# Folding the tokens of a real input twice before its Fourier transform, and writing the outputs in pairs k and N-k

## The reference, cut to what matters

```python
def fourier_mix(u):
    b, n, _ = u.shape
    u32 = u.reshape(b, n, F_GROUPS, F_CH).astype(jnp.float32)
    f = jnp.fft.fftn(u32, axes=(1, 3), norm="ortho").real
    return f.reshape(b, n, F_WIDTH).astype(u.dtype)
```

## Time and profile before

| | |
|---|---|
| median of three runs | 2781.35 us |
| the profiled execution | 2780.91 us |
| its span, first to last instruction | 2779.1 us |
| busy TensorE (matmul) | 2700.9 us, 97% |
| busy VectorE, ScalarE, GpSimd | 1643.2, 1018.4, 968.4 us |
| mean granted TensorE clock | 0.994 |

### The profile page before, as it was taken

How to read it: one execution, slowest core, us unless ns; L and a number is a source line. 1 busy time by engine, 2 the same in 40 slices (tenths; PEclk the granted TensorE clock), 3 DMA queues, 4 the chain that set the end, 5 groups by cost and what they waited for, 6 DMA issues and landing times.

```text
span 2779.1 us, 39815 instructions
## 1 busy us (share of the span) xinstructions
PE 2700.9 (97%) x16386; PEld 2214.9 (80%) x16386; DVE 1643.2 (59%) x1803; ACT 1018.4 (37%) x1377; POOL 968.4 (35%) x596
## 2 busy tenths in 40 slices
PE   7999999999999999999999999999899999999997
PEld 4878877888788888788888888888777888888885
DVE  6479118986963455755436666666869443444436
ACT  4332216773533343445453222222334222222223
POOL 0111115203397873222222111111134744455552
PEclk9999999999999999999999999999999999999998
DMA  7211450012412124111121111111122111111112
GB/s 234 76 31 39 126 185 1 1 65 73 137 46 61 46 61 134 54 48 46 53 57 39 39 39 39 39 39 39 32 77 73 48 46 46 61 61 54 51 31 101
DMA packets 260432, 175.71 MB, mean 63 GB/s; under 512 B 5792, under 2 KB 252960, under 8 KB 259104
## 3 DMA queue, kind: packets, MB, share of 16 engines
q1 hardware_dynamic: 258816, 169.69, 20.3%
q10 hardware_dynamic: 1440, 3.51, 0.3%
HBM read 164.79 MB, written 8.39 MB: 62 GB/s over the span
## 4 chain that ended last, share of the span: by engine, by line
PE 72%; issue 13%; DVE 6%; POOL 4%; ACT 3%; DVEq 1%; DMA 0%; POOLq 0%; SPq 0%; ACTq 0%
PE PS L2134 11%; PE PS L2136 10%; PE PS L2135 10%; PE PS L2537 10%; PE PS L2538 10%; PE PS L2539 10%; POOL Wlo L601 3%; ACT exp L1006 1%; DVE acol L1677 1%; PE PS L2311 1%; PE PS L2641 1%; PE PS L2648 1%; PE PS L2232 1%; PE PS L2448 1%; PE PS L2677 1%
## 5 line engine op out<-in xcount | busy, mean ns | idle before, releaser
L601 POOL TENSOR_TENSOR Wlo<-Wraw,Whi 128x1024 fp32r<-128x1024 f32 (+1 forms) x140 | 337.1, 2408 | 1150.5 <-ACT Whi L795 1150.5
L2134 PE MATMUL PS<-Bh,Whi 128*128 128x512 f32 x1216 | 486.4, 400 | 6.9 <-DVE Bl L1438 2.5
L2136 PE MATMUL PS<-Bh,Wlo 128*128 128x512 f32 x1216 | 475.1, 391 | 0.0
L2135 PE MATMUL PS<-Bl,Whi 128*128 128x512 f32 x1216 | 474.8, 390 | 0.0
L2134 PEld LDWEIGHTS PS<-Bh,Whi 128*128 128x128 f32 x1216 | 228.9, 188 | 60.4 <-DVE Bl L1438 5.9
L2134 PE MATMUL PS<-Hh,Whi 128*128 128x512 f32 x672 | 269.5, 401 | 5.3 <-issue 1.7
L2136 PEld LDWEIGHTS PS<-Bh,Wlo 128*128 128x128 f32 x1216 | 228.9, 188 | 49.4
L2135 PEld LDWEIGHTS PS<-Bl,Whi 128*128 128x128 f32 x1216 | 229.3, 189 | 45.5 <-issue 0.7
L2136 PE MATMUL PS<-Hh,Wlo 128*128 128x512 f32 x672 | 261.8, 390 | 0.0
L2135 PE MATMUL PS<-Hl,Whi 128*128 128x512 f32 x608 | 236.9, 390 | 0.0
L795 ACT ACTIVATE Whi<-Wraw 128x1024 fp32r<-128x1024 f32 (+1 forms) x140 | 144.4, 1031 | 129.7 <-PE PS L2136 127.2
(11 more groups left out here) (436 smaller groups left out, 5867.3 us busy)
## 6 DMA issues: line engine op xcount, KB each, us to landing
Wraw<-in_w_in SPq DMA_DIRECT2D x64, 512.0 KB, 4.1
adaV<-in_ada_w SPq DMA_DIRECT2D x16, 1024.0 KB, 5.3
Wraw<-in_odd_w_in SPq DMA_DIRECT2D x32, 512.0 KB, 4.4
Wraw<-in_w_up SPq DMA_DIRECT2D x32, 512.0 KB, 4.1
Wraw<-in_w_down SPq DMA_DIRECT2D x28, 512.0 KB, 4.3
Wraw<-in_even_w_in SPq DMA_DIRECT2D x24, 512.0 KB, 3.8
adaW<-in_ada_w SPq DMA_DIRECT2D x8, 1024.0 KB, 11.3
Wraw<-in_even_w_out SPq DMA_DIRECT2D x14, 512.0 KB, 3.9
```

The costliest lines, as they stand in the source:

```text
L601: pool.tensor_tensor(Wlo[:, slot, 0:tiles, :], Wraw[:, slot, 0:tiles, :], Whi[:, slot, 0:tiles, :].bitcast(F32), ALU.subtract).then_inc(lo ...
L2134: mm(out, Whi[:, u % 2, k, :], hi[:, k, c], start=(k == 0), stop=False)
L2135: mm(out, Whi[:, u % 2, k, :], lo[:, k, c], start=False, stop=False)
L2136: return mm(out, Wlo[:, u % 2, k, :], hi[:, k, c], start=False, stop=(k == KT - 1))
```

## The change

A real input lets tokens t and N - t be added and subtracted before any transform. The new kernel does that on VectorE, twice: first t with 1024 - t (`fe`, `fo`), then t with 512 - t. That leaves four sets of 256 tokens in `ff`; two need only the channel cosine, two only the channel sine. `chan_dft` then has eight matmuls of 128 columns and one with a stationary operand of a single column (token 256, which pairs with itself). `token_dft` has nine matmuls: cosine of even and odd output frequencies, sine of even and odd ones, two each, and one for the middle token. The outputs k and N - k are the difference and the sum of the cosine and the sine part: ScalarE copies the sine part out of PSUM, VectorE adds and subtracts into `Y` with a step of 2 or -2. The table `token_dft` shrinks from 4096 to 2305 columns. `token_dft(g)` now waits for `fold_copy` of its own group only; `c_root` is awaited there and not in `chan_dft`. The order of the steps on TensorE stays.

```diff
+    uf = at("uf", x0, [2, N + 4])
...
         def uf_out(g):
             got(act, 0, 2, BASE["four"] + g)
             if g >= 2:
-                act.wait_ge(sem("chan_psum"), g - 1)
-            act.activation(uf[:, g % 2, :], acc(g % 2), COPY).then_inc(acc_free[g % 2], 1)
+                act.wait_ge(sem("fold_done"), g - 1)
+            act.activation(uf[:, g % 2, N:N + 1], acc(g % 2)[:, 0:1], COPY)
+            act.activation(uf[:, g % 2, 0:N], acc(g % 2), COPY).then_inc(acc_free[g % 2], 1)
...
+        def sine_copy(g):
+
             act.wait_ge(sem("fourier_psum"), g + 1)
-            act.activation(Y[:, g, :].rearrange("p (n a) -> p a n", a=4), bank(6, N).rearrange("p (a n) -> p a n", a=4),
-                           COPY).then_inc(sem("fourier_out"), 1)
+            act.activation(sines[:, :, :], bank(6, N).rearrange("p (b n) -> p b n", b=2)[:, :, 256:512], COPY).then_inc(sem("sine_copied"), 1)
...
         fold_copy(0)
-        context_modulate()
+        context_modulate(range(4))
         uf_out(2)
         split_next(0, 2, 3)
         fold_copy(1)
-        fourier_out(0)
+        context_modulate(range(4, KT))
+        sine_copy(0)
...
+        def fold(g):
+            dve.wait_ge(acc_free[g % 2], g // 2 + 2)
+            if g >= 2:
+                dve.wait_ge(sem("chan_psum"), g - 1)
+            head, tail = uf[:, g % 2, 0:513], uf[:, g % 2, N:511:-1]
+            tt(fe[:, 0:513], head, tail, ALU.add)
+            tt(fo[:, 0:513], head, tail, ALU.subtract)
+            dve.drain()
+            folds = ff[:, g % 2, 0:N].rearrange("p (f n) -> p f n", f=4)
+            tt(folds[:, 0, :], fe[:, 0:256], fe[:, 512:256:-1], ALU.add)
+            tt(folds[:, 1, :], fe[:, 0:256], fe[:, 512:256:-1], ALU.subtract)
+            tt(folds[:, 2, :], fo[:, 0:256], fo[:, 512:256:-1], ALU.subtract)
+            tt(folds[:, 3, 1:256], fo[:, 1:256], fo[:, 511:256:-1], ALU.add)
+            dve.tensor_copy(folds[:, 3, 0:1], fo[:, 256:257])
+            dve.tensor_copy(ff[:, g % 2, N:N + 1], fe[:, 256:257])
+            dve.drain().then_inc(sem("fold_done"), 1)
+
+        def fourier_out(g):
+
+            ce, co = bank(6, 257), bank(7, 256)
+            se, so = sines[:, 0, 1:256], sines[:, 1, :]
+            dve.wait_ge(sem("sine_copied"), g + 1)
+            tt(Y[:, g, 2:512:2], ce[:, 1:256], se, ALU.subtract)
+            tt(Y[:, g, 1022:512:-2], ce[:, 1:256], se, ALU.add)
+            tt(Y[:, g, 1:512:2], co, so, ALU.subtract)
+            tt(Y[:, g, 1023:511:-2], co, so, ALU.add)
+            dve.tensor_copy(Y[:, g, 0:513:512], ce[:, 0:257:256])
+            dve.drain().then_inc(sem("fourier_out"), 1)
...
+        fold(0)
         dve.wait_ge(sem("c_root"), 1)
         dve.reciprocal(Rc[:, :], Rc[:, :])
-        dve.drain()
+        fold(1)
         for k in range(KT):
             tt(Xc[:, k, :], Xc[:, k, :], Rc[:, :], ALU.mult).then_inc(sem("c_scaled"), 1)
...
+        context_low(range(4))
+        fold(2)
+        context_low(range(4, KT))
+        fourier_out(0)
+        fold(3)
+        fourier_out(1)
+        fourier_out(2)
         dve.memset(vrow[:, :], 0.0).then_inc(sem("rows_cleared"), 1)
         dve.wait_ge(sem("rope_loaded"), 16)
         for c in range(8):
             ph, n, dst, off = ("q", N, qT, 0) if c < 4 else ("k", NK, kT, NC)
+            if c == 1:
+                fourier_out(3)
...
         def chan_dft(g):
-            pe.wait_ge(acc_free[g % 2], g // 2 + 2)
+            pe.wait_ge(sem("fold_done"), g + 1)
             if g == 0:
-                pe.wait_ge(sem("c_root"), 1)
                 pe.wait_ge(sem("m_ready"), 4)
-            if g:
-                pe.wait_ge(sem("fold_done"), g)
+            else:
                 pe.wait_ge(sem("hi_copied"), g)
-            if g >= 2:
-                pe.wait_ge(sem("fourier_out"), g - 1)
-            for t in range(NT):
-                ins = mm(bank(4 + t // 2, 256, (t % 2) * 256), uf[:, g % 2, t * P:(t + 1) * P], chan[:, :], start=True, stop=True)
+            for f in range(4):
+                for t in range(2):
+                    ins = mm(bank(4 + f // 2, P, (2 * (f % 2) + t) * P), ff[:, g % 2, (2 * f + t) * P:(2 * f + t + 1) * P],
+                             chan[:, (f // 2) * P:(f // 2 + 1) * P], start=True, stop=True)
+            ins = mm(bank(5, P)[0:1, :], ff[:, g % 2, N:N + 1], chan[:, 0:P], start=True, stop=True)
             ins.then_inc(sem("chan_psum"), 1)
 
         def token_dft(g):
-            pe.wait_ge(sem("fold_ready"), g + 1)
-            pe.wait_ge(sem("hi_copied"), min(g + 2, GROUPS))
+            pe.wait_ge(sem("hi_copied"), g + 1)
             if g:
                 pe.wait_ge(sem("fourier_out"), g)
-            for a in range(4):
-                for q in range(4):
-                    ins = mm(bank(6, 256, a * 256), Zf[:, g % 2, a, q // 2, q % 2, :], tok[:, q // 2, q % 2, a, :], start=(q == 0), stop=(q == 3))
+            else:
+                pe.wait_ge(sem("c_root"), 1)
+            outs = (bank(6, 257), bank(7, 256), bank(6, 255, 257), bank(7, 256, 256))
+            for f in range(4):
+                n = (257, 256, 255, 256)[f]
+                for t in range(2):
+                    at_t = TOKEN_AT[f] + t * n
+                    ins = mm(outs[f], Zf[:, g % 2, f, t, :], tok[:, at_t:at_t + n], start=(t == 0), stop=(t == 1 and f > 0))
+                if f == 0:
+                    mm(outs[0], Zf[:, g % 2, 2, 0, :], tok[:, TOKEN_AT[4]:TOKEN_AT[4] + 257], start=False, stop=True)
             ins.then_inc(sem("fourier_psum"), 1)
```

More of the change, by code:

```diff
@@ L84, in shape_tables @@
     row = np.arange(256)
-    ang = 2 * np.pi * ((row[:, None] * n[None, :]) % N) / N
-    token = np.stack([np.cos(ang), -np.sin(ang)]).reshape(2, 2, P, 256, 4)
-    token = token.transpose(2, 1, 0, 4, 3).reshape(P, 4096).astype(np.float32)
+    k = np.arange(513)
+    ang = 2 * np.pi * ((row[:, None] * k[None, :]) % N) / N
+    even, odd = ang[:, 0::2], ang[:, 1::2]
+    once = np.where(row == 0, 0.5, 1.0)[:, None]
+    sine_odd = np.where(row[:, None] == 0, np.sin(2 * np.pi * ((256 * k[None, 1::2]) % N) / N), np.sin(odd))
+    middle = np.zeros((P, 257))
+    middle[0] = np.cos(2 * np.pi * ((256 * k[0::2]) % N) / N)
+    by_tile = lambda m: m.reshape(2, P, -1).transpose(1, 0, 2).reshape(P, -1)
+    token = np.concatenate([by_tile(once * np.cos(even)), by_tile(once * np.cos(odd)), by_tile(np.sin(even[:, 1:256])),
+                            by_tile(sine_odd), middle], axis=1).astype(np.float32)
     half = DH // 2
@@ L105, in shape_tables @@
     return {"basic": basic, "chan_dft": chan, "token_dft": token, "rope": rope, "masks": masks}
+TOKEN_AT = (0, 2 * 257, 2 * 257 + 2 * 256, 2 * 257 + 2 * 256 + 2 * 255, 2048)
+TOKEN_COLUMNS = 2048 + 257
 SWAP16 = [i + 16 if i < 16 else i - 16 for i in range(32)]
@@ L188, in build @@
     Hcl = at("Hcl", hc0 + 8 * KB, [KT, NC], F32R)
[L190 to L194, removed]
+    uf = at("uf", x0, [2, N + 4])
+    fe = at("fe", x0 + 8256, [516])
+    fo = at("fo", x0 + 10368, [516])
+    Zf = at("Zf", x0 + 16 * KB, [2, 4, 2, P])
+    sines = at("sines", x0 + 12480, [2, 256])
+    ff = at("ff", x0 + 24 * KB, [2, 4 * 256 + 1])
+    tok = at("tok", x0 + 36 * KB, [TOKEN_COLUMNS])
     chan = at("chan", t0 + 34 * KB, [2 * P])
@@ L898, in context_root, with context_modulate @@
             act.activation(Rc[:, :], bank(6, NC), SQRT, bias=EPSC, scale=1.0 / D).then_inc(sem("c_root"), 1)
-            act.dma_start(tok[:, :, :, :, :].rearrange("p h c a n -> p (h c a n)"), nW["token_dft"]).then_inc(sem("tok_loaded"), 16)
-        def context_modulate():
-            for k in range(KT):
+            act.dma_start(tok[:, :], nW["token_dft"]).then_inc(sem("tok_loaded"), 16)
+        def context_modulate(tiles):
+            for k in tiles:
                 act.wait_ge(sem("c_scaled"), k + 1)
@@ L912, in uf_out @@
             if g >= 2:
-                act.wait_ge(sem("chan_psum"), g - 1)
-            act.activation(uf[:, g % 2, :], acc(g % 2), COPY).then_inc(acc_free[g % 2], 1)
+                act.wait_ge(sem("fold_done"), g - 1)
+            act.activation(uf[:, g % 2, N:N + 1], acc(g % 2)[:, 0:1], COPY)
+            act.activation(uf[:, g % 2, 0:N], acc(g % 2), COPY).then_inc(acc_free[g % 2], 1)
         def fold_copy(g):
             act.wait_ge(sem("chan_psum"), g + 1)
-            act.activation(Zf[:, g % 2, 0:2, :, :, :].rearrange("p a h c n -> p (a h c n)"), bank(6, N), COPY).then_inc(sem("hi_copied"), 1)
-        def fourier_out(g):
+            if g >= 2:
+                act.wait_ge(sem("fourier_psum"), g - 1)
+            act.activation(Zf[:, g % 2, :, :, :].rearrange("p f t c -> p (f t c)"), bank(4, N), COPY).then_inc(sem("hi_copied"), 1)
+        def sine_copy(g):
             act.wait_ge(sem("fourier_psum"), g + 1)
-            act.activation(Y[:, g, :].rearrange("p (n a) -> p a n", a=4), bank(6, N).rearrange("p (a n) -> p a n", a=4),
-                           COPY).then_inc(sem("fourier_out"), 1)
```

(19 more changed lines are left out.)

1 line of the change is left out of this document (removed).

## The result

| | before | after |
|---|---|---|
| median of four runs each, in turns on one chip | 2781.93 us (2780.94 to 2782.52) | 2765.97 us (2763.62 to 2766.43) |
| ratio after / before | | 0.9941, 95% interval 0.9928 to 0.9953 |
| the profiled execution and its span | 2780.91, 2779.1 | 2766.43, 2764.6 |
| mean granted TensorE clock | 0.994 | 0.995 |

The changed kernel is faster by 16.0 us, 0.6%; the forecast was 2763.1, its range 2761.3 to 2767.0. The page's busy line of after, against the earlier trace rows: matmuls last 13.6 us less in sum, on 48 fewer records; VectorE has 20 more instructions and is no busier.

The account below looks back on a forecast made before the run. TensorE's own instructions were taken to set the pace, busy 97% of the span. Terms -17.8 - 1.45 + 0.15 + 0.8 = -18.3 took the profiled 2780.91 to 2762.6, median 2763.1 us; range 2761.3 to 2767.0.

Parts of the forecast that it names:

- Token part: TensorE's token_dft: 2305 columns instead of 4096 take 3.89 us instead of 6.91, saving 3.02 a group, 12.1 in four.
- Rival (e): In token_dft, matmuls of odd width cost double: 8.6 us lost, 2771.7 us; chance 3%.
- Channel part: TensorE's chan_dft: 18 records at 0.112 us take 2.01 instead of 3.45, saving 1.43 a group, 5.7 in four.
- Rival (c): In chan_dft, a 128-column record costs its weight load's 0.192 us: 5.7 us lost, 2768.8 us; chance 3%.
- rival (d): In chan_dft, load and stream run one after the other, 0.304 us a record: 2777.0 us; chance 2%.
- The stall before `token_dft(0)`: TensorE's 1.45 us wait for the second fold_copy ahead of the first token product disappears, as only the first is needed.
- The extra element: ScalarE's uf_out first copies one column from PSUM, delaying TensorE at unit 2 by 0.15 us, bounds 0.1 and 0.2.
- The fold ahead of `chan_dft(0)`: VectorE's first fold, held up by GpSimd's splits, stalls TensorE by 0.8 us; sign: one wait of 0.5 to 1 us.
- (a): In the folds, backward reads cost double: stall at chan_dft(0) 3.4 us, 2.6 more, 2765.7 us; chance 9%.
- (f): In the folds, step -1 reads run at a sixth of the speed: 34.5 us lost, slower at 2797.6; chance 2%.
- rival (b): VectorE becomes the bound in the queries' part, giving back 3.0 us saved in token_dft(3): 2766.1 us; chance 6%.
- rival (g): No gain, because something later waits for a time of its own, a transfer started early: 2781 us; chance 2%.

Follow-up runs that it names:

- the run with the old order alone: Changed kernel with the context's modulation and low parts for all eight tiles in one go again, its relaxed token_dft wait kept; 2764.10 us, ratio 0.9934.
- the run with the later split: Changed kernel with GpSimd waiting for the first fold before it splits unit 3; 2765.28 us, ratio 0.9940, Fourier stretch 70.22 us.
- the other: The changed kernel measured once more with no edit, five runs; 2762.91 us against 2781.39 before, ratio 0.9934.
- the first occasion: The first measurement of the changed kernel against the kernel before, four runs each; 2765.97 us against 2781.93, ratio 0.9941.
- another run: Changed kernel with token_dft waiting again for the next group's fold_copy and all eight context tiles in one go; 2766.09 us, ratio 0.9942.

## Why the prediction was right, point by point

**Token part: right to the hundredth.** 3.89 a group forecast and measured, and 6.93 against 6.91 when columns were added. Rival (e), odd widths at double price, is out.

**Channel part: mechanism right, size off.** The forecast was 2.01 a group by 18 x 0.112, the measurement 2.29, so 1.16 saved a group and not 1.43: 4.6 instead of 5.7. The price of a record was right (0.112 by the run with the products twice, 0.108 for the single column). What the sum left out are 0.28 at three changes of shape, which show when the last of the sixteen records and the second of the single column's stand alone:

```profile
89.80 0.28 PE L2336 MATMUL PS<-chan,ff 128*128 128x128 f32 x1
...
90.12 0.27 PE L2338 MATMUL PS<-chan,ff 128*1 128x128 f32 x1
```

From 88.13 to 89.80 fifteen distances take 1.67, 0.112 each, so entering the row costs nothing. From 89.80 to the first single-column record at 90.01 it is 0.21 and not 0.11; from the second one, at 90.12, to the next projection product at 90.32 it is 0.20 and not 0.11; and that product's own first distance is 0.33 and not 0.23. The term was taken from the middle of a row of 20 equal records, which has no such change. Nor is a change of shape always dear: the 256-column product of before came to 3.45, which is 16 x 0.216, with its way into and out of the row. What makes these three dear was not tested.

Rival (c) had the record at its weight load's 0.192, and rival (d) at load plus stream, 0.304. Sixteen more records cost 1.79 us with loads that last 0.19 each, 3.0 us of loading in 1.8 of time. The Trainium skill's "TensorE: Matmul & The Clock Gate", Part 3, says in one sentence that a load overlaps running matmuls only when it goes to another row group (an earlier one there also allows it for a background weight buffer); these are all loads of the full 128 x 128, and the trace does not agree with that one sentence: by it 64 more records would have cost an estimated 19.5 us, 64 x 0.304 from the rows, and they cost 7.15.

**The stall before `token_dft(0)`: gone, as forecast, and for a reason that is only half of the reason.** The prediction credited the relaxed wait. That it is enough the run with the old order alone shows; but the new order of the context's work would have been enough too, which the prediction did not see: it has no term for that edit.

**The extra element: 0.15 forecast, 0.05 measured.** ScalarE's row for the single column starts at 73.02 and the big copy at 73.07, so the first is nearly hidden beside the second; TensorE's wait for this engine ahead of unit 2 went from 0.96 to 1.02.

**The fold ahead of `chan_dft(0)`: right in kind, a little high.** The forecast had the first add end 0.54 after the split of 1.29, the second and the first quarter add pass freely, the next one held to the end of unit 3's split, and 0.8 of stall. The trace has exactly this order, with 1.61, 0.68, 0.43 and 2.62 us, and the stall's cost is the 0.53 of the run with the later split. The wait itself, 0.31, is shorter than the 0.5 to 1 that the prediction named as its sign. The Trainium skill's "SBUF — State Buffer", section Who interferes with whom, says that a VectorE instruction with two SBUF inputs contends with a GpSimd instruction that reads SBUF, and the one that comes first keeps the shared pair; 2.62 against 0.42 with the split moved away agrees.

**Backward reads: no surcharge.** Rivals (a) and (f) are out by the rows of the first fold. Doubled adds did delay `chan_dft(0)` by 3.05, near the 2.8 that the doubling of streaming and drain comes to, so a surcharge would have been paid there, and with the clock's 2.6 on top, which rival (a), at 2.6 in all, did not have.

**What was costed at nothing:** no new wait of TensorE from unit 2 to unit 6 beside the 0.31, and 259.93 against 259.91 behind it. VectorE's `fourier_out(3)` fits ahead of turn 1 with 1.74 us to spare, so rival (b) is out:

```profile
151.83 0.15 DVE L1632 COPY Y<-PS 128x2 f32<-128x2 f32 x1
153.72 6.55 DVE L1663 RECIPROCAL qR<-qR 128x1024 f32<-128x1024 f32 x1 [1.74 <-ACTq L962]
```

**Sum.** The forecast for the stretch itself, without the extra element ahead of it, was -12.1 - 5.7 - 1.45 + 0.8 = -18.45; it measured -17.72: 1.1 too much taken off for the channel part, 0.3 too much added for the fold, the tokens exact, and the terms so corrected come within 0.1 of it. From the start of unit 6 to the end it is 2618.3 us before, and 2616.9 to 2619.9 in the ten profiles of the changed kernel and its variants, so nothing later gave the gain back, and rival (g) is out as well. Whole executions of the changed kernel then saved 16.0 on one occasion and 18.5 on the other. By the time alone the first occasion's 2765.97 lies nearer to rivals (a), 2765.7, and (b), 2766.1, than to the forecast; it is the rows that rule these out. The difference between the occasions lies outside the Fourier stretch: the same code reached unit 2 at 74.23, 74.35, 72.76 and 72.61 us in four profiled executions whose Fourier stretch was 70.75, 70.74, 70.76 and 70.76, and the attention took 195.3, 195.2, 193.7 and 195.1 there. A stretch after 330 us that changes in length was a sign of being wrong; the attention's 195.30 against 194.25 would be one, but over the ten profiles it took 193.58 to 193.75 in three and 195.05 to 195.30 in seven, on both sides of the one profile of before. Why these two parts vary was not settled, nor whether the change moves their average a little.

## What to carry to other kernels

Price a matmul by the distance between starts in the middle of a row of its own shape, and then look at each change of shape on its own: here three of them cost 0.28 us a block together, while the way into the row cost nothing. Where a change both loosens a wait and moves the work waited for, try each alone and neither: here either would have done. To judge an edit worth a few microseconds, cut the traces at the same instructions, since a stretch repeats to 0.02 us where whole executions scatter by some 4.

## What was not expected of the hardware

- A late operand can cost twice: in a wait of 3.36 us ahead of one `chan_dft` the granted clock fell, and 5.15 us at 0.50 followed, 2.6 us on top of the wait. After the 1.00 us wait of another run, and the 1.45 of before, no such stretch followed.
- GpSimd's split pays for the contention too: 2.64 us beside the fold, 2.39 without it, in addition to VectorE's 2.62 for an add of 0.42. An add was already running when that split started (76.41 and 76.45); the split of the earlier trace rows, which started ahead of the add that it held, took 2.40.
- Of a stationary operand with a single column only the load gets much shorter (0.08 us for 0.19); the distance to the next equal record does not (0.108 for 0.112).
- The granted clock of the profile is not always the speed that the rows show: right after 32.82 us in the changed kernel the projection's products of 512 columns stand 0.43 apart at a listed 1.00, and from 74.54 us on they stand 0.23 apart at the same 1.00.
